# Late modulation rows, band loads, LayerNorm sums and head order of a six-layer transformer kernel rearranged

## The reference

```python
for i in range(DEPTH):
    mod = jax.nn.silu(c) @ ada_w[i] + ada_b[i]
    shift, scale, gate = jnp.split(mod[:, None, :], 3, axis=-1)
    u = x * (1 + scale) + shift
    ...
    x = layernorm(DEEPNORM_ALPHA * x + gate * y, ln_g[i], ln_b[i])
```

```python
mu = xf.mean(-1, keepdims=True)
var = jnp.square(xf - mu).mean(-1, keepdims=True)
return (xf - mu) * lax.rsqrt(var + LN_EPS) * g + b
```

```python
p = jax.nn.softmax(logits, axis=-1)
a = p[:, :, 0] - lam * p[:, :, 1]
o = a @ v
o = _rms(o, subln_g) * (1.0 - lambda_init)
```

## Time and profile before

| | |
|---|---|
| time, median of 3 executions | 3024.41 us (3022.05 to 3027.27) |
| profiled execution, its own time | 3026.88 us |
| its span, first to last instruction | 3025.1 us |
| granted TensorE clock, mean (1 is 2.4 GHz) | 0.965 |
| busy: PE, PEld, DVE | 2835.3, 2340.6, 1517.8 us |
| busy: ACT, POOL | 923.5, 1123.1 us |

### The profile page before, as it was taken

The page is one execution under the profiler, slowest core; times in us unless marked ns, Lnnn a source line. Parts: engine busy times, 40 slices in busy tenths (PEclk is TensorE's granted clock), DMA queues, the critical chain, the costliest instruction groups (busy, mean ns, idle before and its releaser), DMA issues.

```text
span 3025.1 us, 35847 instructions
## 1 busy us (share of the span) xinstructions
PE 2835.3 (94%) x13336; PEld 2340.6 (77%) x13336; DVE 1517.8 (50%) x2043; ACT 923.5 (31%) x1269; POOL 1123.1 (37%) x461
## 2 busy tenths in 40 slices
PE   6699997999899999998999989989999999999998
PEld 5588876778587888877888868867888878788886
DVE  3443357787764744216544046756543065564412
ACT  2233333554312322225222233324222231232222
POOL 1323323212244444441544432314444434344443
PEclk9799998999999999998999999989999999999998
DMA  8743322101133233330333322202333323223332
GB/s 279 232 121 89 108 63 77 56 29 43 59 94 94 82 96 97 104 129 31 111 96 98 100 81 68 76 29 88 105 94 100 99 83 94 87 90 94 96 103 90
DMA packets 106120, 284.92 MB, mean 94 GB/s; under 512 B 38669, under 2 KB 38797, under 8 KB 104675
## 3 DMA queue, kind: packets, MB, share of 16 engines
q1 hardware_dynamic: 98496, 253.14, 27.4%
q10 hardware_dynamic: 7507, 30.14, 2.9%
HBM read 280.98 MB, written 8.85 MB: 96 GB/s over the span
## 4 chain that ended last, share of the span: by engine, by line
issue 63%; POOL 24%; PE 12%; POOLq 1%; DVE 0%; DMA 0%; ACT 0%; ACTq 0%; DVEq 0%
POOL w_lo L546 24%; PE ps L409 4%; PE ps L411 4%; PE ps L410 4%; DMA hot<-in_onehot 0%; POOLq L545 0%; POOLq L164 0%; PE ps L560 0%; DVE x L2049 0%; DVE tmp L2043 0%; PE ps L454 0%; ACT w_hi L402 0%; PE ps L449 0%; PE ps L446 0%; ACTq L1155 0%
## 5 line engine op out<-in xcount | busy, mean ns | idle before, releaser
L546 POOL TENSOR_TENSOR w_lo<-w_raw,w_hi 128x1024 fp32r<-128x1024 f32 x452 | 1122.2, 2487 | 1888.6 <-ACT w_hi L402 1888.1
L409 PE MATMUL ps<-u_hi,w_hi 128*128 128x512 f32 x2240 | 893.2, 399 | 84.4 <-DVE u_lo L1844 39.4
L410 PE MATMUL ps<-u_lo,w_hi 128*128 128x512 f32 x2240 | 883.7, 395 | 0.0
L411 PE MATMUL ps<-u_hi,w_lo 128*128 128x512 f32 x2240 | 882.6, 394 | 0.0
L402 ACT ACTIVATE w_hi<-w_raw 128x1024 fp32r<-128x1024 f32 x452 | 474.6, 1054 | 877.2 <-PE ps L411 792.0
L409 PEld LDWEIGHTS ps<-u_hi,w_hi 128*128 128x128 f32 x2240 | 427.8, 191 | 183.2 <-DVE u_lo L1844 42.4
L410 PEld LDWEIGHTS ps<-u_lo,w_hi 128*128 128x128 f32 x2240 | 428.0, 191 | 89.7 <-issue 1.9
L411 PEld LDWEIGHTS ps<-u_hi,w_lo 128*128 128x128 f32 x2240 | 427.2, 191 | 90.5
L409 PE MATMUL ps<-h_hi,w_hi 128*128 128x512 f32 x704 | 278.3, 395 | 0.0
L411 PE MATMUL ps<-h_hi,w_lo 128*128 128x512 f32 x704 | 278.3, 395 | 0.0
L410 PE MATMUL ps<-h_lo,w_hi 128*128 128x512 f32 x704 | 278.3, 395 | 0.0
(11 more groups left out here) (278 smaller groups left out, 3339.4 us busy)
## 6 DMA issues: line engine op xcount, KB each, us to landing
w_raw<-in_stream SPq DMA_DIRECT2D x452, 512.0 KB, 3.6
late_ring<-in_ada_late ACTq DMA_DIRECT2D x32, 512.0 KB, 5.1
ada_ring<-in_ada SPq DMA_DIRECT2D x8, 1024.0 KB, 7.6
dilated_bias_rows<-dilated_bias ACTq DMA_DIRECT2D x18, 244.1 KB, 6.0
band_a<-dilated_bias_rows SPq DMA_DIRECT2D x96, 28.0 KB, 2.0
x<-in_x SPq DMA_DIRECT2D x8, 256.0 KB, 5.5
bias_rows<-bias_scratch ACTq DMA_DIRECT2D x4, 512.0 KB, 8.2
out_yT<-x SPq DMA_DIRECT2D x8, 256.0 KB, 2.0
```

The lines of the kernel that those rows point to most:

```text
L409: nc.tensor.matmul(o, w[0], v[0], start=start, stop=False)
L410: nc.tensor.matmul(o, w[0], v[1], start=False, stop=False)
L411: return nc.tensor.matmul(o, w[1], v[0], start=False, stop=stop)
L546: nc.gpsimd.tensor_tensor(w_lo[:, s, :], w_raw[:, s, :], w_hi[:, s, :].bitcast(F32), ALU.subtract).then_inc(lo_ready, 1)
```

## The change

It touches four stages.

- **Start and dilated attention.** Late rows are asked for and summed one step later and spread by the tables `LATE_ROWS` and `LATE_REFILLS`. The 18 spread DMAs move from ScalarE to SP, and the bands are loaded in halves by `hh`. `a_project` of the first part no longer waits for `q_evac` and `k_evac`. The sets of late columns stand elsewhere. The four `bias_rows` DMAs follow the rope loads.
- **LayerNorm.** x is scaled earlier, and its last tile is summed from x itself. The mean is read from PSUM. Squares are summed by one-column products, and root and reciprocal are taken of four columns, which four products spread to 128 x 512 again. In layer 0 modulation goes with the tiles.
- **Differential attention.** The first head's values come ahead of its scores; in the others they stand elsewhere. A head's norm goes through columns as well, with the gain multiplied ahead of the factor.
- **Output projection of it.** The last head's two tiles are multiplied one by one as they are ready.

Some removed lines, which stand in the functions above, and the declarations of semaphores are left out.

```diff
--- before.py
+++ after.py
...
-BANDS_AFTER = (3, 5, 8)
...
+LATE_ROWS = ((0, 0, 0, 2, 1, 1, 4), (0, 0, 1, 2, 1, 2, 6), (0, 0, 1, 2, 1, 2, 6))
+LATE_REFILLS = ((0, 0, 0, 0, 2, 1, 1, 1, 1, 1), (0, 0, 1, 1, 2, 1, 2, 1, 2, 1), (0, 0, 2, 1, 2, 1, 2, 1, 2, 0))
...
+            def spread_a(jp):
+                for hh in range(2):
+                    for g in range(NG):
+                        head = HPG * g + 2 * jp + hh
+                        src = bass.AP(a_bias_dram.tensor, head * A_BIAS, [[0, 32], [1, A_BIAS]])
+                        sp.dma_start(a_bias_rows[head], src).then_inc(a_rows[jp], 16)
+            def load_bands(jp, hh):
...
                 if jp:
-                    sp.wait_ge(m_ready, UNITS * jp)
...
+            four(1)
+            sp.wait_ge(a_bias_stored, 16)
+            spread_a(0)
+            load_bands(0, 0)
+            four(2)
+            load_bands(0, 1)
+            spread_a(1)
+            four(3)
+            four(4)
+            load_bands(1, 0)
+            load_bands(1, 1)
+            spread_a(2)
+            for i in range(5, 8):
+                four(i)
+            load_bands(2, 0)
+            load_bands(2, 1)
+            with sp.Fori(8, N_CHUNKS // RING) as i:
...
+            def sum_x_columns(t, b):
+                pe.wait_ge(sqx_ready, n.up("sqx"))
+                for r in range(QB):
+                    mm = pe.matmul(bank(b, 1, at=QB * t + r), sqx[:, t % 2, r * P:(r + 1) * P], ones[:, 0:1],
+                                   start=True, stop=True)
+                mm.then_inc(sqx_summed, 1)
+            def layernorm_sums(layer):
+                pe.wait_ge(acc_ready, n.up("acc"))
+                pe.matmul(bank(7), ones[:, :], acc[:, :], start=True, stop=False)
+                pe.wait_ge(out_evac, KD * (layer + 1))
+                pe.matmul(bank(7), ones[:, :], x[:, KD - 1, :], start=False, stop=True).then_inc(sums_done, 1)
+                for t in range(KD):
+                    sum_x_columns(t, 6)
+                pe.wait_ge(ln_factor, layer + 1)
+                for b in range(QB):
+                    r = bass.AP(col, 12 + b, [[32, P], [0, P]])
+                    mm = pe.matmul(bank(5, P, at=b * P), r, ident[:, :], start=True, stop=True)
+                mm.then_inc(ln_spread, 1)
...
-                pe.wait_ge(k_evac if which else q_evac, NG * jp + g)
                 if jp:
+                    pe.wait_ge(k_evac if which else q_evac, NG * jp + g)
...
-                    pe.wait_ge(late_read, (1, 3, 4)[i // UNITS])
+                    pe.wait_ge(late_read, (1, 2, 4)[i // UNITS])
...
                     for g in (1, 2):
                         a_project(jp, g, 0)
-                        if jp == 1 and g == 1:
-                            late_columns(1)
                         a_project(jp, g, 1)
+                if jp == 2:
+                    late_columns(2)
                 a_values(jp)
                 a_scores(i0)
-                late_columns((0, 2, 3)[jp])
+                late_columns((0, 1, 3)[jp])
...
+            layernorm_sums(0)
...
-                pe.wait_ge(acc_ready, ACC1 + hd + 1)
...
+                for e in range(2):
+                    pe.wait_ge(c_sq, 2 * hd + e + 1)
+                    for b in range(QB):
+                        mm = pe.matmul(bank(7, 1, at=QB * e + b), sq[:, e, b * P:(b + 1) * P], ones[:, 0:1],
+                                       start=True, stop=True)
+                mm.then_inc(c_sums, 1)
+            def head_spread(hd):
+                pe.wait_ge(c_factor, hd + 1)
+                for b in range(QB):
+                    r = bass.AP(col, 12 + b, [[32, P], [0, P]])
+                    mm = pe.matmul(bank(7, P, at=b * P), r, ident[:, :], start=True, stop=True)
+                mm.then_inc(c_spread, 1)
...
-                pe.wait_ge(c_bank_read, unit - 1)
+                pe.wait_ge(c_bank_read, unit - 1 if hd else 1 + half)
...
+                    if b == 2 and hd:
+                        head_spread(hd - 1)
...
+                    pe.wait_ge(o_evac, O1 + LAST)
...
+            c_values(0, 0)
+            c_values(0, 1)
             for hd in range(HC):
...
+                if hd:
+                    c_values(hd, 0)
                 c_scores(hd, 0)
                 if hd:
                     c_pv(hd - 1, 3)
...
+                c_scores(hd, 1)
                 if hd:
                     head_sums(hd - 1)
-                c_scores(hd, 1)
-                c_values(hd, 1)
...
+                else:
+                    c_project(6)
                 c_turn(hd, 0)
                 c_scores(hd, 2)
-                if more:
+                if hd and more:
                     c_project(6 * hd + 6)
-                else:
+                elif not more:
                     pe.wait_ge(c_bank_read, 23)
...
-            pe.wait_ge(o_evac, O1 + HC)
-            for m in range(4):
-                c_out_heads(m, early, KD)
+            head_spread(LAST)
+            for k in range(early, KD):
+                if k == early:
+                    pe.wait_ge(c_half_out, 1)
+                else:
+                    pe.wait_ge(o_evac, O1 + HC)
+                for m in range(4):
+                    c_out_heads(m, k, k + 1)
...
-            act.wait_ge(bias_stored, 16)
-            for jp in range(NJ):
-                spread_a(jp)
...
-                if jp == 0 or g:
-                    late_refills(2)
...
+                late_refills(jp, 2 * g + which)
+            def late_refills(jp, step):
+                for _ in range(LATE_REFILLS[jp][step]):
...
-                    if jp == 0 and g == 2:
-                        act.wait_ge(bias_stored, 32)
...
                     chunk("a_in", A_CH * jp + 2 * NG + c)
-                    if c < 2:
-                        late_refills(2)
+                    late_refills(jp, 2 * NG + c)
...
+                act.wait_ge(ln_means, n.up("ln"))
+                nc.scalar.activation(col[:, 12:12 + QB], col[:, 12:12 + QB], ACT.Sqrt, bias=eps[:, 0:1],
+                                     scale=1.0 / D).then_inc(dev_ready, 1)
...
+            act.wait_ge(bias_stored, 16)
+            for head in range(HC):
+                src = bass.AP(bias_dram.tensor, head * BIAS_W, [[0, P], [1, BIAS_W]])
+                act.dma_start(bias_rows[head], src).then_inc(c_rows, 16)
...
             def c_norm(hd):
                 for e in range(2):
                     act.wait_ge(o_done, T1 + 4 * hd + 4)
...
-                    nc.scalar.activation(sq[:, e, :], bank(2 + e), ACT.Square).then_inc(sq_ready, 1)
-                act_dev(act, n.up("sums"), rs[:, :], 2 * DC, eps_rms)
+                    nc.scalar.activation(sq[:, e, :], bank(2 + e), ACT.Square).then_inc(c_sq, 1)
+                act.wait_ge(c_mean, hd + 1)
+                nc.scalar.activation(col[:, 12:12 + QB], col[:, 12:12 + QB], ACT.Sqrt, bias=eps_rms[:, 0:1],
+                                     scale=1.0 / (2 * DC)).then_inc(dev_ready, 1)
...
-                if jp == 0 or g:
-                    more_rows(2)
...
+                more_rows(jp, 2 * g + which)
+            def more_rows(jp, step):
+                for _ in range(LATE_ROWS[jp][step]):
+                    late_rows(n.up("late") - 1)
...
-                if i % UNITS == 0:
-                    dve.wait_ge(band_landed, 16 * 2 * QB * (QB + 2) * (i // UNITS + 1))
+                if i % QB == 0:
+                    dve.wait_ge(band_landed[hh], 16 * QB * (QB + 2) * (i // UNITS + 1))
...
-                more_rows(4)
-                if jp == 1:
-                    late_mod(1)
+                if jp == 2:
+                    late_mod(2)
+                more_rows(jp, 2 * NG)
                 a_maxima(i0)
-                late_mod((0, 2, 3)[jp])
+                late_mod((0, 1, 3)[jp])
...
+            def residual_scaled(m):
+                ch(nc.vector.tensor_scalar(x[:, m, :], x[:, m, :], ALPHA, None, ALU.mult))
...
+                if m < KD - 1:
...
+                    ins.then_inc(acc_ready, 1) if m == KD - 2 else ch(ins)
+                    residual_scaled(m + 1)
             def layernorm(layer, nxt_scaled):
-                n.up("dev")
...
+                dve.wait_ge(sums_done, (1, 4)[layer])
...
+                    nc.vector.scalar_tensor_tensor(out=x[:, t, :], in0=bank(7), scalar=-1.0 / D, in1=x[:, t, :],
+                                                   op0=ALU.mult, op1=ALU.add).then_inc(x_done, 1)
...
+                c = col[:, 12:12 + QB]
+                dve.wait_ge(sqx_summed, KD * (layer + 1))
+                nc.vector.tensor_reduce(c, bank(6, QB * KD).rearrange("p (t b) -> p b t", b=QB),
+                                        AX.X, ALU.add).then_inc(ln_means, 1)
+                dve.wait_ge(dev_ready, n.up("dev"))
+                nc.vector.reciprocal(c, c).then_inc(ln_factor, 1)
+                dve.wait_ge(ln_spread, layer + 1)
                 for t in range(KD):
...
```

(89 more changed lines are left out.)

96 lines of the change are left out of this document (33 added, 63 removed).

## The result

The changed kernel takes 2975.27 us (median of 4, 2969.79 to 2978.6) against 3025.84 (median of 4, 3022.05 to 3028.0): ratio 0.9832, 95% interval 0.9814 to 0.9851. The forecast was 2970, in a range of 2952 to 2993. The profiled execution took 2976.35 us for a span of 2974.6, 50.5 less than that of before.

The account below looks back on a forecast made before the run. TensorE, busy 2835.3 of 3025.1 us, leaves only 190 us idle and half-clock losses to win. 29.2 + 7.1 - 0.3 + 18.0 = 54.0 off 3026.88 gives 2972.9; set against the median, 2970, range 2952 to 2993 (8 in 10).

Parts of the forecast that it names:

- Start: Start of the dilated attention: earlier third group and second scores, plus clock kept after them; gain 29.2 us, bounds -9 and 32.
- the third group waits only for the copy and its chunk: Start of the dilated attention: TensorE's third product group begins at 75.2 us instead of 88.02.
- Rest of the dilated attention: Later parts of that attention: late rows covered by the products beside them, cost 0; without that cover 4 us.
- LayerNorm 0: LayerNorm of layer 0: product end to product start falls from 31.2 to 24.1 us, gain 7.1, bounds 5.5 and 13.
- rival with a clock that holds: Both LayerNorms: one-column sums run at full clock, 5.8 us less in each; 2958 us, chance 0.15.
- LayerNorm 1: LayerNorm of layer 1: product end to next start 23.3 us instead of 23.0, gain -0.3, bounds -2 and +6.
- Differential attention: Differential attention: gains of first head, heads 1 to 3 and end sum to 18.0 us, bounds 9 and 22.
- Heads 1 to 3: Differential attention: values fill the 2.0 us waits; 13.6 us of losses become 9.4, gain 4.2.
- The end: End of the differential attention: the 8.76 us wait before the last products falls to 5.4, gain 3.4.
- The queue rival: SP's queue at the start: chunk 12 late behind bands and spreads, half the start's gain lost; 2985 us, chance 0.18.
- The slower rival: SP's queue at the start: 60 issues at 2.0 us each eat all 54; at 2.2 the time is 3037; chance 0.03.
- ScalarE's split waits for w_raw in the first 150 us: Start: a sign that would show the prediction wrong, ScalarE waiting for a chunk in that time.

Follow-up runs that it names:

- the kernel with the waits back: The changed kernel with the waits for q_evac and k_evac of the third group's projections put back; 2970.54 us in one run.
- one block of bands: The changed kernel with all 48 bands of the first part and six spreads together on SP between chunks 11 and 12; 2984.84 us.

## Why the prediction held, and where its terms were off

The forecast of 54.0 came within 3.5 of the 50.5, and part of that is luck: terms that were too high by 12.5 in all stand against terms that were too low by 9.0.

- **Start: right in mechanism, 2.5 too much.** The third group came at 75.79, forecast 75.2; the execution ran 0.67 late. Beside that the sum missed by the half clock behind the late columns (3.4 of time by its 6.8 us, I had 2.7) and by the one behind the first wait, which I had left as it was before: the mean clock was 0.70 in the 10 us from 75.79, and before 0.84 in the 10 us from 88.02, 1.4 us of time. With the clock of the kernel with the waits back the gain would have been 31. But of the step "the third group waits only for the copy and its chunk" the wait itself gave 0.1; the rows taken out of the first steps gave what the spreads did not.
- **Rest of the dilated attention: the term I set to 0 was a gain of 6.5.** The late rows were covered as I said. What changed is the half clock: before it fell behind two sets of columns (6.8 us each), after it behind one, for 3.4, which is 5.1 of time; two waits of 0.89 and 0.57 at the start of the third part are gone too. Part of it is chance: in the ten other profiles with the new tables this stretch took 282.3 to 286.1 us (here 282.6, before 289.15 in its one profile), a gain of 3.0 to 6.9.
- **LayerNorm 0: 7.6 for 7.1.** The sums took 12.8 for 13.2, the wait behind the spread 4.3 for 4.3. The rival with a clock that holds did not come in.
- **LayerNorm 1: 1.7 for -0.3, and the step that I left out.** Its sums took 11.2 instead of 13.2. But the half clock lasts past the stage: the convolution behind it took 2.7 longer, of which 1.0 is the start at half clock (5.7 us of it against 3.6) and 1.7 a further dip of 3.4 us from 791.8 on, found in ten of the 13 profiles of changed kernels, for which no run shows the cause.
- **Differential attention: 11.4 for 18.0, the largest miss.** No run undoes its head order or norms; this is read from the traces. The first head gave 9.9 for 10.4. Heads 1 to 3 gave 1.9 for 4.2: the wait for m_lo, which I let shrink from 3.3 to 1.3 by a shorter chain, stayed:

```profile
1935.34 0.17 DVE L2258 RECIPROCAL col<-col 128x2 f32<-128x2 f32 x1 [1.70 <-ACT pc L1575]
...
1939.83 5.13 POOL L573 TENSOR_TENSOR w_lo<-w_raw,w_hi 128x1024 fp32r<-128x1024 f32 x2 [19.93 <-ACT w_hi L412]
...
1940.53 2.19 DVE L2286 TENSOR_TENSOR m_lo<-tmp,m_hi 128x512 fp32r<-128x512 f32 x1
...
1942.87 0.76 PE L419 MATMUL ps<-m_hi,w_hi 128*128 128x512 f32 x1 [3.30 <-DVE m_lo L2286]
```

  The chain lost its 3.35 reciprocal, but `c_outputs` now stands behind the head's second softmax, whose exponential VectorE awaits for 1.70 and whose passes take 1.6: together as long as the reciprocal, under which that exponential had run. ScalarE's table loads have little part in it: the first softmax waits 1.59 without one. And the last m_lo took 2.19 us beside GpSimd's w_lo, where the m_lo at 1938.36 took 0.69 (before it was 1.79, also beside a w_lo), so 1.5 of the 3.30 is this. The end gave -0.4 for 3.4: the wait did fall (5.7 with the longer sums and the spread in it, for 8.76; forecast 5.4), and the 2.79 for w_lo with its half clock, which the sum did not have, took it back.
- **Rivals.** The queue rival's place was real (one block of bands costs 7.2 us at the second scores), but at 0.59 an issue there were 7 us of cover. The slower rival's 2.0 per issue never came near. The lower end of the range, 2952, is 2 below what its own parts give, 2958 less 4.
- **The sign of being wrong was badly chosen.** "ScalarE's split waits for w_raw in the first 150 us" did happen, for 9.53 us at 108.80 (and for 12.7 before), and cost TensorE nothing: ScalarE was ahead of it and had that time to spare. The wait of TensorE for va, which came back in the kernel with one block of bands, was the sign to name.

## What to carry to other kernels

Cost a moved release as well as a moved product: going by k instead of by m freed the ring slot late, and the next chunk's split, behind a square that nobody hurried, became the wait; with the split ahead of the square that stage was the shortest of the three that ran. When several edits stand before one wait, undo them in pairs: here the wait that the change names was worth 0.1 us, and the rows that were queued behind it 8 or more. And one-column products won nothing here even at full clock, 0.95 us a tile against 0.96 for the 128x512 sum; at half clock they took 1.70, and the LayerNorms with 128x512 sums were 2 to 4 us faster each, reciprocal included.

## What the runs showed of the hardware

- Among one-column products the granted clock fell even with TensorE busy 94% of the stage by records (0.73 over 25.1 us), while in 128x512 sums at the same place it stayed at full: 7.70 us for eight tiles without a pause, for which the sums of before took 9.1.
- The dips are not fixed by the order: behind the same sixteen one-column products the clock fell for 6.8 us in the changed kernel's profile and in nine others not at all, 3.4 us of time. Two profiles of kernels with the same start may differ by that much, so a difference of this size between single profiles can't be put down to an edit.
- A pass of VectorE over two SBUF tiles of 128x512 took 0.69 us alone and 2.19 beside GpSimd's subtraction for w_lo (1.79 in the kernel before).
- The 24 band DMAs between two groups of chunk loads (16 of 28 KB, 8 of 16 KB) were issued at 0.58 us each, against 0.71 for the 48 of before.
